# Latent queries and keys made turned by the weights, with only their rotated columns turned by themselves

## The reference

```python
qb = jnp.einsum('bsr,re->bse', rmsnorm(cq, q_norm), w_q_up).reshape(bt, n, H_B, NOPE_B + ROPE_B)
kvb = jnp.einsum('bsr,re->bse', rmsnorm(ckv, kv_norm), w_kv_up).reshape(bt, n, H_B, NOPE_B + V_B)
...
qbr = axial_rope(qbr, rows, cols)
kr = axial_rope(kr[:, :, None, :], rows, cols)[:, :, 0, :]
...
o_b = mla_latent(qbn, qbr,
                 jnp.concatenate([kbn_c, kbn], axis=1),
                 jnp.concatenate([kr_c, kr], axis=1),
                 jnp.concatenate([vb_c, vb], axis=1))
```

## Time and profile before

| | |
|---|---|
| median of three runs | 3214.45 us |
| lowest, highest | 3212.38, 3215.31 us |
| the profiled execution | 3210.73 us |
| its span | 3209.0 us |
| TensorE busy | 3045.9 us, 95% |
| VectorE, ScalarE, POOL busy | 48%, 25%, 26% |
| mean granted clock of TensorE | 0.978 of full |
| the four blocks of the change | from 384.04 to 473.28 us |
| the latent attention | from 473.28 to about 777 us |

### The profile page before, as it was taken

One profiled execution on the slowest core, in us unless ns is written; L12 is line 12 of the kernel. 1 busy time (PEld: TensorE's weight loads), 2 busy tenths in 40 slices (PEclk: granted clock), 3 DMA queues, 4 the chain that ended last, 5 costly groups with the idle time before them and its releaser, 6 DMA issues. The chain is left out here.

```text
span 3209.0 us, 36884 instructions
## 1 busy us (share of the span) xinstructions
PE 3045.9 (95%) x14466; PEld 1727.5 (54%) x14466; DVE 1533.5 (48%) x2532; ACT 810.7 (25%) x1658; POOL 833.2 (26%) x660
## 2 busy tenths in 40 slices
PE   7999999999959999799999999999999999999999
PEld 4456656665424444344456657444445666665444
DVE  2345437776451111524322465313768777775234
ACT  3226525443211111412211126211011222221001
POOL 0005401012100100023022215412616665451323
PEclk9999999999979999899999999999999999999999
DMA  7210000001287897511000130012211122117433
GB/s 296 78 55 28 1 27 1 18 10 55 79 339 301 333 345 247 182 40 40 30 24 28 54 138 2 33 40 79 88 70 56 63 79 79 73 46 285 163 129 137
DMA packets 72315, 334.55 MB, mean 104 GB/s; under 512 B 10960, under 2 KB 12496, under 8 KB 58320
## 3 DMA queue, kind: packets, MB, share of 16 engines
q1 hardware_dynamic: 67536, 315.42, 25.9%
q0 software_dynamic: 4608, 16.78, 2.1%
HBM read 283.92 MB, written 48.23 MB: 104 GB/s over the span
## 5 line engine op out<-in xcount | busy, mean ns | idle before, releaser
L3383 PE MATMUL banks<-down_ring,down_sums 128*128 128x512 f32 x440 | 191.1, 597 | 4.7 <-DVE down_ring L3410 4.7
L849 PE MATMUL banks<-kT_b,qT_b_and_w_out 96*128 96x512 f32 (+1 forms) x384 | 158.8, 523 | 3.7 <-ACT prob_b L911 2.4
L3085 PE MATMUL banks<-hT,ffn_raw 128*128 128x512 f32 x352 | 157.6, 601 | 2.4 <-PEq L2571 1.3
L329 PE MATMUL banks<-w_in,hT 128*128 128x512 f32 (+1 forms) x384 | 157.1, 567 | 1.2 <-PEq L157 1.2
L3201 DVE SCALAR_TENSOR_TENSOR ffn_acc<-ffn_u,s_ffn_taps,ffn_acc 128x1023 f32<-128x1023 f32 x88 | 131.5, 1505 | 30.4 <-ACT ffn_acc L3138 28.8
L3383 PEld LDWEIGHTS banks<-down_ring,down_sums 128*128 128x128 f32 x440 | 84.1, 191 | 111.4 <-issue 104.2
L733 POOL TENSOR_TENSOR prob<-prob,softmax_columns 128x640 f32<-128x640 f32 (+1 forms) x64 | 75.5, 1201 | 261.9 <-DVE softmax_columns L689 261.9
L1806 PE MATMUL banks<-hT,side_ring 128*128 128x512 f32 x256 | 126.7, 614 | 1.3 <-PEq L2358 1.3
L1453 PE MATMUL banks<-expert_wg,expert_xT 128*128 128x512 f32 x256 | 115.1, 603 | 2.4 <-ACT expert_xT L1490 1.7
L1532 DVE TENSOR_TENSOR expert_h<-banks,expert_silu 128x512 f32<-128x512 f32 x16 | 11.1, 691 | 219.6 <-ACT expert_silu L1499 219.6
L329 PEld LDWEIGHTS banks<-w_in,hT 128*128 128x128 f32 x384 | 71.9, 190 | 77.9 <-issue 77.9
(11 more groups left out here) (625 smaller groups left out, 6141.8 us busy)
## 6 DMA issues: line engine op xcount, KB each, us to landing
down_ring<-in_w_down SPq DMA_DIRECT2D x132, 256.0 KB, 2.9
expert_wg<-in_w_gate SPq DMA_DIRECT2D x16, 2048.0 KB, 15.3
expert_wu<-in_w_up SPq DMA_DIRECT2D x16, 2048.0 KB, 20.7
expert_wd<-in_w_down SPq DMA_DIRECT2D x16, 2048.0 KB, 8.6
ffn_raw<-in_w_ffn SPq DMA_DIRECT2D x22, 1024.0 KB, 6.2
wmod_slab<-in_w_mod SPq DMA_DIRECT2D x6, 2048.0 KB, 7.9
act_rows<-ffn_acc SPq DMA_DIRECT2D x22, 512.0 KB, 2.7
act_rows<-act_rows SPq DMA_DIRECT2D x22, 512.0 KB, 8.7
```

The costliest lines, as they stand in the source:

```text
L329: last = nc.tensor.matmul(c.ps[:, base + a:base + b], h[:, q, :], k.w_in[i][:, q, 0:b - a], start=q == 0, stop=q == KD - 1)
L849: last = nc.tensor.matmul(scores(u)[:, a:b], heads[u // 2].q[u % 2], heads[u // 2].keys[u % 2][:, a:b], start=True, stop=True, skip_group_ ...
L3085: last = nc.tensor.matmul(c.bank(fi), wt[:, q, :], x[:, q, :], start=q == 0 and m != 2, stop=q == 3, skip_group_check=True)
L3383: return nc.tensor.matmul(c.bank(4 * (p % 2) + t), stationary_of(s)[:, P * t:P * t + P], w[s % RING][:, 0, :], start=j == 0, stop=j == N - 1)
```

## The change

The first four of the five blocks become one, `project_latent`. Queries and keys are computed with the weights as the stationary operand and the turned latents as the moving one, so the plain columns of two heads come out turned, 128 rows to a bank. The rotated columns of the queries are still computed by token, 256 columns for two tiles to a bank, rotated by VectorE straight from the bank into `q_rope`, and turned at the end: 4 pairs of heads times 8 tiles. The shared rotated key is spread by POOL into 96 columns, turned once for each of 10 tiles and copied to all heads. The order of bank uses is: 4 of rotation (two tiles each), 10 of values, 3 of the shared key, 12 of keys, 8 of queries, 8 of rotated queries. TensorE waits for the use eight places before.

Of each bank with plain columns ScalarE takes the rows 0 to 63 for the even head of the pair and VectorE the rows 64 to 127 for the odd head. So an even head has its plain columns in rows 0 to 63 and the rotated ones in 64 to 95; an odd head has the rotated ones in rows 0 to 31, zeros in 32 to 63 and plain ones in 64 to 127. `heads` slices 96 rows for even heads and 128 for odd ones. The places of `v_b`, `kT_b`, `prob_b` and `probT_b` in memory change, and the columns of `w_q_up` are put in another order when the inputs are laid out.

The lines taken out of `project_up` are left out here, since the function stands above.

```diff
@@ -474,73 +474,143 @@
                 last.then_inc(scaled, 1)
-def project_up(c, k, d, which):
+def project_latent(c, k, kr4, q_rope):
     nc = c.nc
...
+    made, rotated, spread, act_out, dve_out, link = (c.sem(f"up_{s}") for s in ("made", "rotated", "spread", "out_act", "out_dve", "link"))
+    PAIRS, SCALE = HB // 2, QKB ** -0.5
+    CUTS = [(0, 512), (512, 1024), (1024, NK * P)]
+    uses = ([("rotate", t) for t in range(0, NT, 2)] + [("value", t) for t in range(NK)] + [("key_rope", cut) for cut in CUTS]
+            + [("key", i, cut) for i in range(PAIRS) for cut in CUTS] + [("query", i, a) for i in range(PAIRS) for a in (0, 512)]
+            + [("query_rope", i, a) for i in range(PAIRS) for a in (0, 512)])
+    by_act, by_dve = [], []
+    for kind, *at in uses:
+        by_act.append((by_act[-1] if by_act else 0) + (kind != "rotate" and (kind != "value" or at[0] % 2 == 0)))
+        by_dve.append((by_dve[-1] if by_dve else 0) + (kind != "rotate" and (kind != "value" or at[0] % 2 == 1)))
+    def bank(n):
+        return c.bank(n % 8)
     with nc.Block(no_gpsimd_drain=True) as block:
+        @block.gpsimd
+        def _(pool):
+            nc.gpsimd.memset(q_rope[:, :, :, 0, 32:64], 0.0).then_inc(spread, 1)
+            nc.gpsimd.memset(kr4[:, :, 32:64], 0.0).then_inc(spread, 1)
+            for at in (0, 64):
+                nc.gpsimd.tensor_copy(kr4[:, :, at:at + ROPE], k.kr_key[:, :, :]).then_inc(spread, 1)
         @block.tensor
         def _(pe):
...
+            pe.wait_ge(k.up_in["q"], 16)
+            for n, (kind, *at) in enumerate(uses):
+                if n >= 8:
+                    if uses[n - 8][0] == "rotate":
+                        pe.wait_ge(rotated, uses[n - 8][1] + 2)
+                    else:
+                        pe.wait_ge(act_out, by_act[n - 8])
+                        pe.wait_ge(dve_out, by_dve[n - 8])
+                if kind == "rotate":
+                    for t in (at[0], at[0] + 1):
+                        for q in range(KQ):
+                            last = nc.tensor.matmul(bank(n)[:, 256 * (t % 2):256 * (t % 2) + 256], k.cqT[:, q, P * t:P * t + P], k.w_q_up[:, q, 512:768],
+                                                    start=q == 0, stop=q == KQ - 1, skip_group_check=True)
+                elif kind == "key_rope":
+                    pe.wait_ge(spread, 4)
+                    a, b = at[0]
+                    for t in range(a // P, b // P):
+                        last = nc.tensor.transpose(bank(n)[0:96, P * t - a:P * t - a + P], kr4[:, t, :], k.ident[:, :])
+                elif kind == "query":
+                    i, a = at
+                    for q in range(KQ):
+                        last = nc.tensor.matmul(bank(n), k.w_q_up[:, q, P * i:P * i + P], k.cqT[:, q, a:a + BANK], start=q == 0, stop=q == KQ - 1)
+                elif kind == "query_rope":
+                    i, a = at
+                    pe.wait_ge(rotated, a // P + 4)
+                    for t in range(4):
+                        last = nc.tensor.transpose(bank(n)[0:96, P * t:P * t + P],
+                                                   q_rope[:, a // P + t, i, :, :].rearrange("p s n -> p (s n)")[:, 0:96], k.ident[:, :])
+                elif kind == "key":
+                    i, (a, b) = at
+                    for q in range(KKV):
+                        last = nc.tensor.matmul(bank(n)[:, 0:b - a], k.w_kv_up[:, q, P * i:P * i + P], k.ckvT[:, q, a:b], start=q == 0, stop=q == KKV - 1)
+                else:
+                    if at[0] == 0:
+                        pe.wait_ge(k.up_in["kv"], 16)
+                    for q in range(KKV):
+                        last = nc.tensor.matmul(bank(n), k.ckvT[:, q, P * at[0]:P * at[0] + P], k.w_kv_up[:, q, 512:1024], start=q == 0, stop=q == KKV - 1)
+                last.then_inc(made, 1)
         @block.scalar
         def _(act):
...
+            for n, (kind, *at) in enumerate(uses):
+                if kind == "rotate" or kind == "value" and at[0] % 2:
+                    continue
+                act.wait_ge(made, n + 1)
+                if kind == "key_rope":
+                    a, b = at[0]
+                    src = bank(n)[0:64, 0:b - a].unsqueeze(1).to_broadcast([64, PAIRS, b - a])
+                    ins = nc.scalar.activation(k.kT_b[0:64, 1:HB:2, a:b], src, ACT.Identity)
+                elif kind == "query":
+                    i, a = at
+                    ins = nc.scalar.activation(k.qT_b[0:64, 2 * i, a:a + BANK], bank(n)[0:64, :], ACT.Identity, scale=SCALE)
+                elif kind == "query_rope":
+                    i, a = at
+                    ins = nc.scalar.activation(k.qT_b[0:64, 2 * i + 1, a:a + BANK], bank(n)[0:64, :], ACT.Identity, scale=SCALE)
+                elif kind == "key":
+                    i, (a, b) = at
+                    ins = nc.scalar.activation(k.kT_b[0:64, 2 * i, a:b], bank(n)[0:64, 0:b - a], ACT.Identity)
                 else:
...
+                    act.wait_ge(spread, 4)
+                    ins = nc.scalar.activation(k.v_b[:, at[0], :], bank(n), ACT.Identity)
+                ins.then_inc(act_out, 1)
         @block.vector
         def _(dve):
             step = Chain(dve, link)
...
+            def rotate(n, t):
+                src = bank(n)[:, 256 * (t % 2):256 * (t % 2) + 256]
+                out, o4 = k.tmp[:, 256:512], k.tmp[:, 0:256].rearrange("p (h a s f) -> p h a s f", h=HB, a=2, s=2)
+                s4 = src.rearrange("p (h a s f) -> p h a s f", h=HB, a=2, s=2)
+                table = k.rope_b[:, t]
+                if t:
+                    dve.wait_ge(rotated, t)
+                step.put(nc.vector.tensor_tensor(out.rearrange("p (h e) -> p h e", h=HB), src.rearrange("p (h e) -> p h e", h=HB),
+                                                 table[:, 0, :].unsqueeze(1).to_broadcast([P, HB, ROPE]), ALU.mult))
+                sin = table[:, 1, :].rearrange("p (a s f) -> p a s f", a=2, s=2)
+                for s in range(2):
+                    step.put(nc.vector.tensor_tensor(o4[:, :, :, s, :], s4[:, :, :, 1 - s, :],
+                                                     sin[:, :, s, :].unsqueeze(1).to_broadcast([P, HB, 2, 8]), ALU.mult))
+                step.wait()
+                nc.vector.tensor_tensor(q_rope[:, t, :, :, 0:ROPE], out.rearrange("p (i s e) -> p i s e", i=PAIRS, s=2),
+                                        k.tmp[:, 0:256].rearrange("p (i s e) -> p i s e", i=PAIRS, s=2), ALU.add).then_inc(rotated, 1)
+            for n, (kind, *at) in enumerate(uses):
+                if kind == "value" and at[0] % 2 == 0:
+                    continue
+                dve.wait_ge(made, n + 1)
+                if kind == "rotate":
+                    for t in (at[0], at[0] + 1):
+                        rotate(n, t)
+                    continue
+                if kind == "key_rope":
+                    a, b = at[0]
+                    src = bank(n)[64:96, 0:b - a].unsqueeze(1).to_broadcast([32, PAIRS, b - a])
+                    ins = nc.vector.tensor_copy(k.kT_b[64:96, 0:HB:2, a:b], src)
+                elif kind == "query":
+                    i, a = at
+                    ins = nc.vector.tensor_scalar(k.qT_b[64:128, 2 * i + 1, a:a + BANK], bank(n)[64:128, :], SCALE, None, ALU.mult)
+                elif kind == "query_rope":
+                    i, a = at
+                    ins = nc.vector.tensor_scalar(k.qT_b[64:96, 2 * i, a:a + BANK], bank(n)[64:96, :], SCALE, None, ALU.mult)
+                elif kind == "key":
+                    i, (a, b) = at
+                    ins = nc.vector.tensor_copy(k.kT_b[64:128, 2 * i + 1, a:b], bank(n)[64:128, 0:b - a])
                 else:
...
+                    dve.wait_ge(spread, 4)
+                    ins = nc.vector.tensor_copy(k.v_b[:, at[0], :], bank(n))
+                ins.then_inc(dve_out, 1)
 class Pair:
@@ -1000,22 +1070,13 @@
     attend_pairs(c, k, "window", pairs, bufs, before=up_weights)
 
 
-    k.b_tok = c.area("b_tok", F + 6720, NK, HB, QKB)
     qT_and_w = c.area("qT_b_and_w_out", F + 30464, HB, SEQ)
-    k.qT_b = qT_and_w[0:QKB, :, :]
-    project_up(c, k, d, "q")
-    groups = [([k.b_tok[:, t, h, :] for t in g(t0)], k.qT_b[:, h, P * t0:P * t0 + BANK], QKB ** -0.5, None)
-              for t0 in (0, 4) for h in range(HB)]
-    transpose_groups(c, "turn_qb", groups, k.ident)
-    k.v_b = c.area("v_b", F + 14400, NK, 512)
-
-    project_up(c, k, d, "kv")
-    k.kT_b = c.area("kT_b", F + 19520, HB, NK * P, parts=QKB)
-    groups = [([k.b_tok[:, t, h, :] for t in ts], k.kT_b[:, h, P * ts[0]:P * ts[0] + P * len(ts)], None, None)
-              for ts in ([0, 1, 2, 3], [4, 5, 6, 7], [8, 9]) for h in range(HB)]
-    transpose_groups(c, "turn_kb", groups, k.ident)
-    bufs = (c.area("prob_b", F + 5440, 3, NK * P), c.area("probT_b", F + 9280, 2, 2, NK * P), c.area("softmax_columns_b", F, 4, 3, 2))
```

(35 more changed lines are left out.)

35 lines of the change are left out of this document (removed).

## The result

| | before | after |
|---|---|---|
| median of four runs | 3213.41 us | 3192.97 us |
| lowest, highest | 3211.34, 3215.31 | 3191.72, 3194.05 |
| the profiled execution | 3210.73 | 3194.05 |
| its span | 3209.0 | 3192.3 |
| ratio, 95% interval | | 0.9936 (0.9919 to 0.9954) |

The change is faster, as forecast, but by more: 20.4 us in the medians where 14.3 were forecast, and 3192.97 lies under the range of 3195 to 3205. The two profiled executions are 16.7 us apart.

What follows compares the result with a forecast made beforehand. TensorE, busy 95% of the span, was taken as the bound. Fewer turnings and handovers, less the end-of-block wait, gain 16.0 us; less 1.7 for a clock fall, 14.3: from 3214.45 to 3200.1 us, range 3195 to 3205.

Steps and rivals of the forecast that it cites:

- The stage: From the first latent-query product to the first latent-attention scores, 89.24 us: gains 16.0 us, 14.3 after a clock fall.
- Prices and products: Query, key and value products, priced per TensorE record: 65.79 us against 65.77 before, so nothing won or lost.
- Turnings: Transpositions of queries and keys: 144 taking 17.74 us become 42 at 0.111, 4.66 us.
- Handovers: Between the blocks of the stage: four become one; the gaps of 2.65, 1.11 and 1.12 us go.
- Evictions inside the block: Copies out of banks by ScalarE and VectorE, and POOL's work, stay covered under TensorE's products and cost nothing.
- both rivals: Engines sharing a bank hinder each other: 3206, chance 0.10; odd heads' 128-row products are dearer: 3220.7 at 30%, chance 0.04.
- The end of the block: VectorE's last nine copies take 5.9 us behind the last query product, leaving TensorE idle 2.75 us before the first scores.
- The clock at the attention's start: After the 2.75 us gap the clock falls and the first scores take 1.7 us more, counted in full.
- clock kept: Rival at the handover into the attention: the clock does not fall, gain 16.0 us, 3198.4 us; chance 0.28.
- Everything later shifts: Code behind the stage only starts earlier: no transfer is under way across the stage; no gain or loss counted there.
- a few gaps later in the kernel: Later gaps at lengths where the clock sometimes falls, with the 3 us run spread: 2 us on each side of every case.
- The anchor: Starting time for the forecast: median of three runs, 3214.45 us, 3.7 above the profiled 3210.73; gives 3200.1.

Runs made afterwards that it cites:

- e6: The changed kernel cut into four blocks, nothing else moved: stage 240.8 us against 236.6 with the clock held; mean 3198.0 us against 3192.7.
- e9: The kernel before, unchanged, profiled once more to count clock falls: stage 253.2 us, outside it 2958.8 us.
- e11: The kernel before, unchanged, profiled again to count clock falls: stage 253.3 us, outside it 2958.2 us.
- e8: The changed kernel, unchanged, profiled a third time: stage 236.6 us, outside it 2952.9 us.
- e5: The kernel before with 18 transpositions of the identity in the gap at 415.24: stage 251.7 us; mean of eleven runs 3210.4 us against 3212.8.

## Why the prediction was wrong

- The stage. Prices and products: right. 66.48 us measured for the 66.9 of the sum, the difference being mostly the 0.16 us by which a last record outlasts the distance to a next one; my prices (whole stretches divided by their records) counted it in both product stretches. Turnings: 3.66 for 3.55, and 0.110 each when added alone. Handovers: e6 says 4.3 us in place of the 2.3 to 3.0 for three of them. Evictions inside the block: TensorE waits for none. The shared key took 2.28 and 1.86 us per copy for 2.3 and 2.1 expected; POOL 2.0 us for 3.1. Neighbouring rows of one bank don't disturb each other, and 128 rows cost what 96 do: both rivals fell.
- The end of the block: right in mechanism, shorter by 0.3 us. The nine copies took 5.53 us, for 5.9.
- The clock at the attention's start: this step was wrong in kind. I took one outcome, a fall, for 1.7 us. Measured it varies from execution to execution: a fall in two of five traces, worth 2.2 us, since the clock was down from the first record and not from 0.46 us on. Without it the stage gains 16.7 us (forecast 16.0), with it 14.4; the mean is 15.8. The rival "clock kept" had 0.28 and was the more frequent case; with the delayed kernels, whose gap is the same, it is 5 of 12. The evidence that I took for it was no better: the gap of 2.26 us ahead of 1811.81, behind which the clock held, is followed by 0.60 in two of the four traces of before (e9, e11).
- The step that failed is "Everything later shifts", which took the time of the later code as fixed. It shifts and changes its length: 3.8 us of the 19.6 are gained outside the stage, in the traces mostly behind gaps after which the clock falls more rarely, or comes back sooner, than in before. The latent attention itself is not where it happens: from its first scores to the next block's first product it takes 306.0 us before and 305.7 in e8. I had allowed 2 us on each side for "a few gaps later in the kernel". There are eleven gaps of 2.2 to 4.7 us behind the attention's start in the first trace of before, one stretch alone swings by 6.9 us between executions, and the mean moved by up to 4 us when the code was delayed. Why the falls come as they do is open.
- The anchor. The sum was set on the median of three runs, 3214.45. The mean of the 82 later executions is 3212.3, so 2.2 us of the miss are there. I had noted that the profiled execution was 3.7 us under the median and added all of it back, though nothing in the profile explained it.

The miss of 7.1 us (3200.1 to 3192.97) is therefore 1.5 us in the stage, 3.8 outside, 2.2 in the anchor, less 0.4 of rounding and chance. The sign and the mechanism of the gain in the stage were right (that its sum came so near in the first profile, 14.4 for 14.3, was luck in part: the block gained 0.6 us more than forecast and the fall cost 0.5 more); the range was too narrow because it was built on the stage's terms and treated the rest of the kernel as fixed.

## What to carry to other kernels

Where TensorE bounds, an operand that comes out of the product in the orientation in which it is needed is worth the full price of the turnings it saves, and fewer blocks are worth their handovers; both can be summed from two or three stretches of the trace. Put last in a block the work whose copies keep up with TensorE: 3.7 us of turnings with 5.5 us of copies leave a gap of 2.5, one product with one copy a gap of 1.1. A forecast for a kernel with many idle times of 2 to 4 us on TensorE needs several microseconds of range for the clock alone, and an anchor from more than three runs.

## What the runs showed of the hardware that I had not expected

- After a gap of 2.46 us the clock fell in two traces and held in three of the same kernel; behind 2.13 us it held in two and fell in three; behind 1.12 us or less it held in every trace at the end of the stage. A fall at the attention's start cost 2.2 us.
- Falls at different gaps go together: in the scan the gaps of 3.23 and 2.26 us were both followed by a fall in seven traces and neither in thirteen.
- Transpositions alone ran at 2.4 GHz (8.91 us at 1.00), and 2.0 us of transpositions of the identity put into the gap of 2.65 us were followed by 1.00, where four traces without them had the slow clock (e5).
- With a delay of 8.9 and 11.2 us the unchanged later code took 3.7 and 4.1 us more (errors 0.9 and 0.8), the stage's own end included.
- A handover between blocks cost TensorE 0.39 us behind the last copy in before and in the change, and 0.65 in e6, where the next list began with waits on several semaphores; that the waits are the cause is not shown.
